# Paired filter of a causal convolution: one tap a product through diagonal weights, or four taps a product through shifted copies of the rows

## The reference, cut to what matters

```python
def conformer_conv_module(x, prev, w_glu, b_glu, w_dw, b_dw, ln_g, ln_b, w_out, b_out):
    a, g = jnp.split(x @ w_glu + b_glu, 2, axis=-1)
    u = a * jax.nn.sigmoid(g)
    u_ext = jnp.concatenate([prev.astype(u.dtype), u], axis=1)
    c = depthwise_causal_conv(u_ext, w_dw) + b_dw
    c = jax.nn.silu(layer_norm(c, ln_g, ln_b))
    return c @ w_out + b_out, u_ext[:, -(CONV_A_WIDTH - 1):]
```

## Time and profile before

| | before |
|---|---|
| median of 3 runs (lowest to highest) | 3170.02 us (3169.92 to 3171.07) |
| span of the profiled execution, first to last instruction | 3167.7 us |
| GLU stage: u of block 0 starts, u of block 7 starts | 58.41 us, 285.10 us |
| PE, DVE, ACT busy over the span | 98%, 64%, 44% |

### The profile page before, as it was taken

How to read it: one execution, slowest core, us unless ns; L and a number is a source line. 1 busy time by engine, 2 the same in 40 slices (tenths; PEclk the granted TensorE clock), 3 DMA queues, 4 the chain that set the end, 5 groups by cost and what they waited for, 6 DMA issues and landing times.

```text
span 3167.7 us, 67410 instructions
## 1 busy us (share of the span) xinstructions
PE 3115.2 (98%) x27396; PEld 2826.8 (89%) x27396; DVE 2037.0 (64%) x3090; ACT 1383.0 (44%) x2300; POOL 194.2 (6%) x351
## 2 busy tenths in 40 slices
PE   8999899999999999999999999999999999999998
PEld 7888899999999999999766666666799999999998
DVE  6999777753565445643678777877666763465533
ACT  5333643233333333323667777767543223333332
POOL 0000000000000002231101000110000000000000
PEclk9999999999999999999999999999999999999999
DMA  4110223333333335556899999999633333333332
GB/s 119 32 44 26 60 81 88 93 91 108 107 111 91 90 104 162 161 180 193 321 379 383 383 385 391 388 392 369 240 87 91 90 88 103 115 102 97 94 103 88
DMA packets 476789, 525.23 MB, mean 166 GB/s; under 512 B 20369, under 2 KB 397834, under 8 KB 476280
## 3 DMA queue, kind: packets, MB, share of 16 engines
q1 hardware_dynamic: 463286, 477.91, 44.9%
q0 software_dynamic: 13104, 42.83, 4.0%
q10 hardware_dynamic: 92, 0.19, 0.0%
HBM read 486.90 MB, written 33.95 MB: 164 GB/s over the span
## 4 chain that ended last, share of the span: by engine, by line
PE 87%; DVE 8%; ACT 2%; issue 2%; DMA 1%; SPq 0%; DVEq 0%; POOL 0%; ACTq 0%; POOLq 0%
PE PS L986 59%; PE PS L2062 8%; PE PS L2098 4%; PE PS L2075 4%; DVE mT L821 4%; PE PS L2113 3%; PE PS L2123 2%; PE PS L2132 2%; PE PS L346 1%; DVE wlo L336 1%; PE PS L2084 1%; PE PS L567 1%; ACT whi L332 1%; PE PS L1608 1%; PE PS L543 1%
## 5 line engine op out<-in xcount | busy, mean ns | idle before, releaser
L336 DVE TENSOR_TENSOR wlo<-raw,whi 128x1024 fp32r<-128x1024 f32 x368 | 450.6, 1224 | 574.9 <-ACT whi L332 561.4
L332 ACT CAST whi<-raw 128x1024 fp32r<-128x1024 f32 x368 | 386.2, 1049 | 972.4 <-PE PS L986 933.4
L986 PE MATMUL PS<-xfh,whi 128*128 128x264 f32 (+1 forms) x3072 | 631.1, 287 | 1.1 <-DVE wlo L336 1.1
L986 PE MATMUL PS<-xfl,whi 128*128 128x264 f32 (+1 forms) x3072 | 625.5, 285 | 0.0
L986 PE MATMUL PS<-xfh,wlo 128*128 128x264 f32 (+1 forms) x3072 | 624.0, 284 | 0.0
L986 PEld LDWEIGHTS PS<-xfh,whi 128*128 128x128 f32 x3072 | 479.2, 188 | 5.0 <-issue 2.1
L986 PEld LDWEIGHTS PS<-xfl,whi 128*128 128x128 f32 x3072 | 478.8, 188 | 0.0
L986 PEld LDWEIGHTS PS<-xfh,wlo 128*128 128x128 f32 x3072 | 478.4, 188 | 0.0
L986 PE MATMUL PS<-pA,whi 128*128 128x264 f32 x2048 | 333.0, 284 | 0.0
L986 PEld LDWEIGHTS PS<-pA,whi 128*128 128x128 f32 x2048 | 282.4, 188 | 0.4
L2062 PE MATMUL PS<-ident,kr 128*128 128x128 f32 x2048 | 276.7, 276 | 0.3 <-ACT kt L2193 0.3
(11 more groups left out here) (335 smaller groups left out, 5133.5 us busy)
## 6 DMA issues: line engine op xcount, KB each, us to landing
kr<-in_cache_k SPq DMA_DIRECT2D x256, 512.0 KB, 6.4
vr<-in_cache_v SPq DMA_DIRECT2D x256, 512.0 KB, 6.4
raw<-in_ffn_w_gate SPq DMA_DIRECT2D x88, 512.0 KB, 3.8
raw<-in_ffn_w_up SPq DMA_DIRECT2D x88, 512.0 KB, 3.9
raw<-in_ffn_w_down SPq DMA_DIRECT2D x64, 512.0 KB, 4.1
raw<-in_ffn_w_down SPq DMA_DIRECT2D x32, 384.0 KB, 3.4
raw<-in_conv_w_glu SPq DMA_DIRECT2D x16, 512.0 KB, 3.9
raw<-in_conv_w_out SPq DMA_DIRECT2D x16, 512.0 KB, 3.9
```

Source lines behind the costliest of these rows:

```text
L332: nc.scalar.copy(whi[b][:], raw[b][:]).then_inc(w_hi, 1)
L336: nc.vector.tensor_tensor(wlo[b][:], raw[b][:], whi[b][:].bitcast(F32), ALU.subtract).then_inc(w_lo, 1)
L986: mm = nc.tensor.matmul(PS[:, s + c, 0:c1 - c0], wt[t % RING][:, kw + k, :], x(k0 + k)[:, c0:c1], start=start and k == 0 and wt is whi and ...
```

## The change

All 16 paired taps of every block go to PE, four taps a matmul. Four copies of the pair sums, each shifted by one more column, are laid under each other: for a group g of 32 features, `shifted` holds on partitions 32s to 32s+31 the pair sums of these features shifted by s columns. A weight block `quads` of 128 x 32 then holds four taps for 32 features, and 4 groups x 4 steps = 16 matmuls of 128 x 32 weights and 512 columns give the filter. The copies are 16 DMAs of 32 partitions x 524 columns (67 KB) a block, issued by SP between weight loads; pair sums move to the front of DVE's work on a block; DVE's six paired taps are gone; DVE and no longer ACT reads PE's sum out of PSUM, in `last_close` too; ACT makes 16 blocks of 32 columns for 10 diagonals of 128.

```diff
-PE_TAPS = (10, 10, 10, 10, 10, 10, 10, 16)
 EV = 16
+QUAD = 4
+ZW = 512 + EV - QUAD
...
-    diag0 = at("diag0", [P, 10, P], F32, TB_AT + 2 * ROW)
-    diag1 = at("diag1", [P, 6, P], F32, TB_AT + 2 * ROW + 5120)
-    diag2 = at("diag2", [P, 8, P], F32, O2 + 8 * UP + 7680 + 1536 + 1088)
+    shifted = at("shifted", [P, 4, ZW], F32, TB_AT + 2 * ROW)
+    quads = [at(f"quads{j}", [P, 4, EV // QUAD, 32], F32, O2 + 8 * UP + 7680 + 1536 + 1088 + 2048 * j) for j in range(2)]
...
         def glu_sp(sp):
-            for m in range(1, KB):
-                load_tile(sp, 2 * m, 0, cols(w_glu, KB + m), KB)
-                load_tile(sp, 2 * m + 1, 1, cols(w_glu, m), KB)
+            def weights(t):
+                if t < 2 * KB:
+                    load_tile(sp, t, t % RING, cols(w_glu, (1 - t % 2) * KB + t // 2), KB)
+                else:
+                    load_tile(sp, t, t % RING, cols(A["conv_w_out"][0], t - 2 * KB), KB)
+
+            def shifts(m):
+                sp.wait_ge(g_z, m + 1)
+                if m >= 1:
+                    sp.wait_ge(g_tap, m)
+                for s in range(QUAD):
+                    for g in range(4):
+                        sp.dma_start(shifted[32 * s:32 * s + 32, g, :], pair_sums(m)[32 * g:32 * g + 32, s:s + ZW]).then_inc(g_sh, 16)
+
+            for t in range(2, 5):
+                weights(t)
+            for m in range(KB):
+                shifts(m)
+                for t in (2 * m + 5, 2 * m + 6):
+                    if t < 2 * KB + OUT_EARLY:
+                        weights(t)
...
         def glu_pe(pe):
-            def gate_or_value(m, b):
-                if m >= 1:
+            def gate_or_value(m, b, k0=0, k1=KB):
+                if k0 == 0:
                     pe.wait_ge((g_sig, g_ev)[b], m)
-                product(pe, 2 * m + b, b, b, KB, 0, xh, xl, CH, True, True)
+                    pe.wait_ge(w_lo, 2 * m + b + 3)
...
             def taps(m):
-                pe.wait_ge(g_z, m + 1)
+                pe.wait_ge(g_sh, SH * (m + 1))
                 pe.wait_ge(g_dg, m + 1)
                 if m >= 1:
                     pe.wait_ge(g_cin, m)
-                for j in range(PE_TAPS[m]):
-                    a = EV - PE_TAPS[m] + j
-                    mm = nc.tensor.matmul(PS[:, 6, :], diag(m, j), pair_sums(m)[:, a:a + 512], start=j == 0, stop=j == PE_TAPS[m] - 1)
-                mm.then_inc(g_tap, 1)
+                quad_taps(m, 6, 0, 512).then_inc(g_tap, 1)
+
+            def quad_taps_spread():
+
+                pe.wait_ge(g_wz, 2)
+                pe.wait_ge(g_wr, 1)
+                pe.wait_ge(st_a, 2)
+                for g in range(4):
+                    for s in range(QUAD):
+                        mm = nc.tensor.matmul(PS[32 * s:32 * s + 32, 7, 32 * g:32 * g + 32], ident[:, 32 * g:32 * g + 32],
+                                              bass.AP(wz, s, [(KB * EV, P), (EV, KB), (QUAD, EV // QUAD)]), start=True, stop=True,
+                                              skip_group_check=True)
+                mm.then_inc(g_w4, 1)
...
             pe.wait_ge(x_rt, 4)
             first_pair()
+            quad_taps_spread()
             for m in range(KB):
                 if m + 1 < KB:
                     gate_or_value(m + 1, 0)
-                if m == 0:
-                    pe.wait_ge(st_a, 2)
-                if m < KB - 1:
                     taps(m)
                     gate_or_value(m + 1, 1)
...
-        def last_taps_pe(pe, h, j0, j1):
-
...
+        def last_taps_pe(pe, h):
+
             if h == 0:
-                pe.wait_ge(g_z, KB)
-                pe.wait_ge(g_dg, KB + 1)
+                pe.wait_ge(g_sh, SH * KB)
+                pe.wait_ge(g_dg, KB)
                 pe.wait_ge(g_cin, KB - 1)
-            for j in range(j0, j1):
-                mm = nc.tensor.matmul(PS[:, 6 - h, 0:n1 - n0], diag(m, j), pair_sums(m)[:, j + n0:j + n1], start=j == 0, stop=j == EV - 1)
-            if j1 == EV:
-                mm.then_inc(g_tap, 1)
-
-        def last_taps_out(act, h):
-            n0, n1 = LAST[1][h]
-            act.wait_ge(g_tap, KB + h)
-            if h == 0:
-                act.wait_ge(g_cv, KB - 1)
-            nc.scalar.activation(mT[:, KB - 1, 2 * n0 + 1:2 * n1:2], PS[:, 6 - h, 0:n1 - n0], ACT.Identity,
-                                 bias=vec[:, KB - 1, V_BDW:V_BDW + 1]).then_inc(g_cin, 1)
+            quad_taps(KB - 1, 6 - h, *LAST[1][h]).then_inc(g_tap, 1)
...
             m, (o0, o1) = KB - 1, LAST[1][h]
             odd, both = mT[:, m, 2 * o0:2 * o1:2], mT[:, m, 2 * o0 + 1:2 * o1:2]
             dve.wait_ge(g_dve, glu_steps[0])
+            dve.wait_ge(g_tap, KB + h)
+            nc.vector.scalar_tensor_tensor(out=both, in0=PS[:, 6 - h, 0:o1 - o0], scalar=vec[:, m, V_BDW:V_BDW + 1],
+                                           in1=second(m, o0 + 1, o1 + 1), op0=ALU.add, op1=ALU.subtract).then_inc(g_cin, 1)
             dve.wait_ge(g_cin, KB + h)
-            glu_then(nc.vector.tensor_tensor(both, both, second(m, o0 + 1, o1 + 1), ALU.subtract))
-            dve.wait_ge(g_dve, glu_steps[0])
             glu_then(nc.vector.tensor_tensor(both, both, odd, ALU.subtract))
             nc.vector.scalar_tensor_tensor(out=odd, in0=odd, scalar=vec[:, m, V_BDW:V_BDW + 1], in1=second(m, o0, o1),
...
+        SH = 16 * 4 * QUAD
+
+        def quad_taps(m, bank, n0, n1):
+
+            for j in range(EV // QUAD):
+                for g in range(4):
+                    mm = nc.tensor.matmul(PS[32 * g:32 * g + 32, bank, 0:n1 - n0], quads[m % 2][:, g, j, :],
+                                          shifted[:, g, QUAD * j + n0:QUAD * j + n1], start=j == 0, stop=j == EV // QUAD - 1,
+                                          skip_group_check=True)
+            return mm
...
-        def diagonals(act, m, j0, j1):
+        def quad_weights(act, m):
             if m >= 2:
-                act.wait_ge(g_tap, m - 1 if j0 == 0 else m)
-            for j in range(j0, j1):
-                a = EV - PE_TAPS[m] + j
-                ins_ = nc.scalar.activation(diag(m, j), ident[:], ACT.Copy, scale=wz[:, m, a:a + 1])
-            if j1 == min(14, PE_TAPS[m]) or j0 == 14:
-                ins_.then_inc(g_dg, 1)
+                act.wait_ge(g_tap, m - 1)
+            for g in range(4):
+                for j in range(EV // QUAD):
+                    ins_ = nc.scalar.activation(quads[m % 2][:, g, j, :], pick4[:], ACT.Copy, scale=wq4[:, g, m, j:j + 1])
+            ins_.then_inc(g_dg, 1)
...
-            def taps_out(m):
-                act.wait_ge(g_tap, m + 1)
-                nc.scalar.activation(mT[:, m, 1:NP:2], PS[:, 6, :], ACT.Identity, bias=vec[:, m, V_BDW:V_BDW + 1]).then_inc(g_cin, 1)
...
             value(0)
             split_hi(act, 3, 1, 1)
             act.wait_ge(st_a, 2)
+            act.wait_ge(g_w4, 1)
+            nc.scalar.copy(wq4[:].rearrange("p g m j -> p (g m j)"), PS[:, 7, 0:P]).then_inc(g_wr, 1)
             for m in range(2):
                 states_in(m)
-            diagonals(act, 1, 0, 10)
+            act.wait_ge(g_wr, 2)
+            for m in range(2):
+                quad_weights(act, m)
             for m in range(KB):
                 tails(m)
                 first_taps(m)
                 if m + 1 < KB:
                     gate(m + 1)
                     split_hi(act, 2 * m + 4, m + 2, 0)
-                if m < KB - 1:
-                    taps_out(m)
-                if m + 2 < KB:
-                    diagonals(act, m + 2, 0, min(14, PE_TAPS[m + 2]))
-                if m == KB - 2:
-                    diagonals(act, KB - 1, 14, 16)
                 if m + 1 < KB:
                     value(m + 1)
                     split_hi(act, 2 * m + 5, m + 2, 1)
                 states_out(m)
                 if m + 2 < KB:
+                    quad_weights(act, m + 2)
                     states_in(m + 2)
...
+                dve.wait_ge(g_u, m + 1)
+                if 1 <= m < KB - 1:
+                    dve.wait_ge(g_sh, SH * m)
+                if m == KB - 1:
+                    dve.wait_ge(g_ut, m)
+                nc.vector.tensor_tensor(pair_sums(m), us[:, 1:1055:2], us[:, 2:1056:2], ALU.add).then_inc(g_z, 1)
                 if m < KB - 1:
                     split_lo(dve, 2 * m + 3, 1)
-                    samples(dve, m, second(m, 0, NS * CW))
-                dve.wait_ge(g_u, m + 1)
-                if m < KB - 1:
-                    dve.wait_ge(g_sd, m + 1)
-                if m == KB - 1:
-                    dve.wait_ge(g_tap, m)
-                    dve.wait_ge(g_ut, m)
-                nc.vector.tensor_tensor(pair_sums(m), us[:, 1:1055:2], us[:, 2:1056:2], ALU.add).then_inc(g_z, 1)
-
+                    samples(dve, m, sig[:, 0:NS * CW])
...
-                n = EV - PE_TAPS[m]
...
+                for a in range(1, EV):
...
-                    if 0 <= paired < n:
-                        if paired == 0:
-                            dve.wait_ge(g_cin, m + 1)
```

(51 more changed lines are left out.)

13 lines of the change are left out of this document (4 added, 9 removed).

## The result

The changed kernel takes 3183.34 us, median of 4 runs (3179.56 to 3184.93); the kernel before took 3170.33 beside it (3169.92 to 3171.07). The ratio is 1.0040 with a 95% interval of 1.0028 to 1.0053: slower by 13 us, where 10 us less were forecast. The profiled execution of the changed kernel is the fastest of its four, 3179.56 with a span of 3177.8; before it was 3167.7. So the traces account for 10.1 of the 13 us, and for 20.3 of what lies between forecast and result (3177.8 against 3167.7 - 10.2 = 3157.5).

A forecast was written before the change was run, and what follows sets the result against it. DVE was taken to set the GLU blocks' pace, with PE 1.4 us ahead and both full; +0.4 - 19.2 + 0 + 6.9 + 1.7 = -10.2 on the 3170.0 median gave 3160, range 3153 to 3171.

The forecast's parts named there:

- DVE's block, 29.1 us: DVE's GLU block: six paired taps leave (-3.98), moved pair sums +0.73, close +0.05; 32.3 becomes 29.1 us.
- PE's taps, 3.5 us in place of 8.6: PE in each GLU block: 32 narrow records, four at a time, take 3.5 us where ten diagonals took 8.59.
- Rival C: Narrow matmuls run one after the other: PE 37.5 us a block, 3215 with the stall; chance 0.03.
- The loop, 18.8 + S: From one u through pair sums, copies, taps, value product and readout to the next: 27.3 us, hidden by DVE's 29.1.
- S = 8.5: Time from pair sums until the last of 16 copies lands: 0.43 us an issue, 2.0 landing; bounds 7.4 to 10.6.
- rival A: Copies come late, PE waits: blocks pay above 10.3 us, break-even 11.6 (0.64 an issue), 3182 at 0.75; chance 0.16.
- rival D: ACT is the bound: 0.30 us a weight block, or PE's clock falls before the taps; 3162 to 3166; chance 0.09.
- ACT's chain, "1.1 us of slack": ACT in each block, readout through 16 weight blocks (3.8 us): ready at 33.5, 1.1 us before DVE's sample sums.
- The first close, "just hidden": After block 7: copies and narrow taps take 14.2 us, hidden under 14.7 us of DVE's own taps; no cost.
- worth 0 to 0.7: Block 7's second taps on PE get shorter, ahead of the layer norm's squares: gain 0 to 0.7 us, taken as 0.
- The third tile's wait, +6.9: Output product's third tile: PE waits for DVE's second close to read out the last taps' bank, +6.9 us.
- the clock behind it, +1.7: PE's clock at 0.57 after idling, in the output product behind the third tile's wait: +1.7 us, bounds 0 and 3.5.

The follow-up runs named there:

- experiments 1: Changed kernel without the 128 shifted copies, narrow taps reading the pair sums themselves (part of the computation left out): 3158.86 us, ratio 0.9964.
- experiment 3: Two runs on the changed kernel: copies split over SP's and POOL's queues, 3159.98 us; three of eight value-product rows ahead of the narrow taps, 3162.78.
- experiment 5: Changed kernel, second half's sum read by ACT, block 1's weight blocks later, plus value product partly ahead (3152.02), copies on two queues (3146.49), or both (3148.74).
- Experiment 4: Changed kernel with block 7's second-half tap sum read out by ACT again: 3173.87 us; kernel before with that readout by DVE's second close: 3181.49.
- experiment 5, first run: Changed kernel with three eighths of the value product ahead, second half's sum read by ACT, block 1's weight blocks made later: 3152.02 us, ratio 0.9941.

## Why the prediction was wrong, step by step

- **DVE's block, 29.1 us**: right. Where the copies don't bind (experiments 1, 3 and 5) u to u is 29.1 to 29.3 us, but for one block of 29.38 and, where ACT makes 32 weight blocks first, block 0 with 32.2. DVE's first tap then waits 1.03 us for ACT, where "+0.62" and "+0.1" had been put.
- **PE's taps, 3.5 us in place of 8.6**: right, 3.64 at full clock. No gap of a change between wide and narrow matmuls shows; 3.64 us after the taps start the value product does. Rival C falls.
- **The loop, 18.8 + S with "S = 8.5"**: this step failed, in the size of one term. The form was right: 18.8 + 11.58 = 30.4 against 30.70 measured. The landing was right too, 2.0. The issue was not: 0.43 us was taken, between 0.37 and 0.54 from loads with other shapes, and it is 0.63 from start to start. 15 x 0.63 + 2.1 = 11.5, beyond even the upper bound of 10.6. At 0.54 the loop would have taken an estimated 29.4 (30.70 - 15 x 0.09), next to nothing over DVE's pace; at 0.63 every steady block pays 1.6 us. That is rival A's mechanism, at its own point of decision ("S = 11.6, 0.64 us an issue"). The rows of loads were treated as a bound, though none of them moves 32 partitions inside SBUF, which the prediction itself said. Which property of the copies makes an issue 0.63 us is not shown: the runs vary their bytes and their queue, not their partitions.
- **What the gap does to the clock**: a part of rival D, priced there at 1.7 us for a chain through ACT and not added to A. Here it adds to A, as the wait is on the path. The steady 1.6 us in six blocks make 9.6, block 0 is 1.0 over its forecast (its taps take 6.19), and the rest of the 15.0 is nearly all in blocks 1 and 2, 1.3 and 3.0 over 30.70. Block 1's is the clock, taps of 4.92 in place of 3.64. Of block 2's, 1.7 is the clock (5.34) and 1.3 the one slow issue, which no rival had. So A at its break-even, which its formula put at no change, came out 10 to 13 us slower.
- **ACT's chain, "1.1 us of slack"**: right in size (16 weight blocks in 3.51 us, 0.22 each, forecast 0.235); in the steady block ACT was still 0.2 us early. The 32 of block 0 took 6.92, and DVE's first tap came 9.68 after u(0) for 10.7. There ACT is the bound as soon as the copies are not: block 0 takes 32.2 us in experiments 1 and 3, and 29.2 with 16 of the 32 made later.
- **The first close, "just hidden"**: wrong, as it hung on the same S. The copies land at 13.5 after u(7) and PE's taps start there, at the low clock behind 9.14 us of idle time (3.75 us for 264 columns); the close comes at 299.78 - 282.33 = 17.45 us for 14.7, +2.75. The other 1.2 us come from the second half's taps, "worth 0 to 0.7" and taken as 0. All 32 records of them now stand ahead of block 7's mean, where 10 of 32 stood before, so the mean and behind it DVE's centring start later. Before, then after:

```profile
301.17 1.27 PE L873 MATMUL PS<-mT,mean 128*128 128x264 f32 x4 [3.17 <-DVE mT L642]
302.47 2.55 DVE L923 TENSOR_TENSOR mT<-mT,PS 128x528 f32<-128x528 f32 x4 [0.20 <-PE PS L873]
...
303.23 1.16 PE L872 MATMUL PS<-mT,mean 128*128 128x264 f32 x4
304.43 2.54 DVE L922 TENSOR_TENSOR mT<-mT,PS 128x528 f32<-128x528 f32 x4 [2.11 <-PE PS L872]
...
307.74 3.83 PE L888 MATMUL PS<-sq,mean 128*128 128x264 f32 x8 [3.35 <-DVE sq L912]
```

  DVE loses 1.96 us there, had 0.73 of slack further on, and starts its reciprocal 1.2 late. The squares on PE (last row) run at the low clock, 3.83 us for 1.94, and their result is ready at the same moment (315.87, with DVE free at 315.93), so either would have cost this alone.
- **The third tile's wait, +6.9, and the clock behind it, +1.7**: right in place and nearly in size, 6.70 and, over two tiles, 14.20 - 11.84 = 2.4. Experiment 4 gives 9.5 for the two by the medians, 9.0 by the traces.

## What to carry to other kernels

A new loop through transfers (result, copy, use) is only as short as the queue that issues them: count the issues, multiply by the time from start to start of an issue of the same shape, and take rows of other shapes as no bound where the answer turns on a fifth of it (here 0.54 or 0.63 us). If the loop is near the pace of the busiest engine, plan from the start for two queues (and for a longer landing with both at work, here 3 us for 2) or for independent work in front of the waiting instruction. And an engine that gives up a readout to a busier one moves the release of its buffer to that one's queue, here from 309.3 to 343.6 us; that alone cost 9 us, where the seven blocks gained 3.8.

## Unexpected of the hardware

- An SBUF-to-SBUF copy of 32 partitions takes SP's queue 0.59 us to issue with 65.5 KB and with 32.8 KB alike (16 in 10.02 us both times), 0.63 from start to start for the 0.54 of the loads in the earlier trace rows. GpSimd's queue issued the same copies every 0.49 us, faster than SP.
- In blocks 0 and 2 of every trace with all 16 issues on SP they take 10.8 to 11.5 us and not 10.0. The traces do not show why.
- A copy lands in 2.0 us, or 1.9 with half the bytes, when SP alone issues, and in 3.2 (SP) and 2.8 (GpSimd) when both do. The Trainium skill, "DMA: Bandwidth & Descriptors", section Anatomy of one DMA, gives some 2.0 us fixed plus bytes by 436 GB/s for a DMA issued by GpSimd, an estimated 2.15 here; GpSimd's copies took 2.8, and no run has them without SP's beside them.
- A gap of 3.24 us on PE left its clock at 1.00 in some blocks, and one of 3.27 was followed by taps of 4.92 us for 3.64. Even gaps of 1.95 and 2.52 us were followed by 5.34 us at a clock of 0.68 (experiment 5, first run), and another of 2.52 by 3.64 us at 1.00 (experiment 3, value product ahead). The same program differed from execution to execution (three to five slow blocks). What decides it these runs do not show.
